# Product of activations and gates moved from VectorE to GpSimd, with each chunk's gathers behind it

## What is computed

```
s = einsum('nhpc,hpkc->nhpk', q, keys32)          # 8 heads, 2 x 128 keys
top_s, top_i = lax.top_k(s, 16)
cand_s = top_s[:, :, 0, :, None] + top_s[:, :, 1, None, :]
best_s, best_c = lax.top_k(cand_s.reshape(n, 8, 256), 16)
expert_idx = take_along_axis(cand_i, best_c)      # 128 experts per position
gate = softmax(best_s)
act = gelu(einsum('nhkd,nd->nhk', expert_u[expert_idx], x_blk))
out = einsum('nhk,nhkd->nd', gate * act, expert_v[expert_idx])
```

## Time and profile before

| what | value |
|---|---|
| median of 3 runs | 1731.21 us (1728.63 to 1732.78) |
| the profiled execution | 1731.74 us |
| its span in the trace | 1730.0 us |
| PE busy | 1696.1 us, 98% of the span |
| DVE busy | 1295.1 us, 75% |
| ACT busy | 774.3 us, 45% |
| POOL busy | 770.5 us, 45% |
| granted clock of TensorE, 1400 to 1500 us | 1.00 |
| DMA share, 1400 to 1500 us | 0.99 |

### The profile page before, as it was taken

The page is one execution under the profiler, slowest core; times in us unless marked ns, Lnnn a source line. Parts: engine busy times, 40 slices in busy tenths (PEclk is TensorE's granted clock), DMA queues, the critical chain, the costliest instruction groups (busy, mean ns, idle before and its releaser), DMA issues.

```text
span 1730.0 us, 24584 instructions
## 1 busy us (share of the span) xinstructions
PE 1696.1 (98%) x9066; PEld 1513.9 (88%) x9066; DVE 1295.1 (75%) x1838; ACT 774.3 (45%) x1101; POOL 770.5 (45%) x486
## 2 busy tenths in 40 slices
PE   7999999989999999999999999999999999999998
PEld 5888788878899999999999999999888888888886
DVE  2555511135999999989999789886787887878886
ACT  5555422333333566756666566654323323223233
POOL 3333243423311556655556678881533433433330
PEclk9999999999999999999999999999999999999999
DMA  5222223322335777687777988898999999999992
GB/s 158 74 73 85 61 82 100 97 73 73 96 119 203 245 243 249 231 287 253 248 253 250 334 310 300 309 308 314 372 380 379 359 362 375 359 362 375 360 378 76
DMA packets 212438, 413.80 MB, mean 239 GB/s; under 512 B 11521, under 2 KB 150817, under 8 KB 207009
## 3 DMA queue, kind: packets, MB, share of 16 engines
q1 hardware_dynamic: 156880, 253.51, 42.4%
q0 software_dynamic: 36864, 134.23, 21.6%
q10 hardware_dynamic: 18640, 25.45, 4.2%
HBM read 360.73 MB, written 52.43 MB: 239 GB/s over the span
## 4 chain that ended last, share of the span: by engine, by line
PE 81%; DVE 9%; POOL 4%; issue 2%; DMA 2%; ACT 1%; ACTq 0%; SPq 0%; POOLq 0%; DVEq 0%
PE psum L1226 30%; PE psum L233 22%; PE psum L1167 20%; PE psum L1157 3%; DVE ring L1500 2%; POOL ring L1384 2%; DVE ul L1425 2%; PE psum L1194 2%; PE psum L308 1%; POOL grid L1403 1%; DVE hot L1488 1%; PE psum L434 1%; POOL hot L1394 1%; DVE hot L1490 1%; DMA ring<-in_expert_u,index 1%
## 5 line engine op out<-in xcount | busy, mean ns | idle before, releaser
L1167 PE MATMUL psum<-xTh,uh 128*128 128x384 f32 x1024 | 354.2, 346 | 5.1 <-DVE ul L1425 4.4
L1167 PE MATMUL psum<-xTh,ul 128*128 128x384 f32 x1024 | 343.3, 335 | 0.0
L1167 PE MATMUL psum<-xTl,uh 128*128 128x384 f32 x1024 | 343.3, 335 | 0.0
L216 POOL TENSOR_TENSOR wl<-raw,wh 128x1024 fp32r<-128x1024 f32 x72 | 173.5, 2420 | 307.1 <-ACT wh L497 307.1
L1384 POOL DMA_INDIRECT ring<-in_expert_v,index x128 | 174.7, 1365 | 296.9 <-DVE acc L1505 253.7
L1226 PE MATMUL psum<-vh,dwh 128*128 128x512 f32 x768 | 298.8, 389 | 1.2 <-DVE dwl L1518 1.2
L1226 PE MATMUL psum<-vh,dwl 128*128 128x512 f32 x768 | 298.8, 389 | 0.0
L1226 PE MATMUL psum<-vl,dwh 128*128 128x512 f32 x768 | 298.8, 389 | 0.0
L1299 ACT ACTIVATE vh<-v_raw 128x4096 fp32r<-128x4096 f32 x31 | 112.6, 3633 | 340.2 <-PE psum L1226 339.8
L1384 POOL DMA_INDIRECT ring<-in_expert_u,index x128 | 178.1, 1391 | 153.2 <-DVE ring L1500 79.5
L1500 DVE SCALAR_TENSOR_TENSOR ring<-ring,x 128x1024 f32<-128x1024 f32 x120 | 199.9, 1678 | 9.3 <-DMA ring<-in_expert_u,index 8.0
(11 more groups left out here) (209 smaller groups left out, 2880.5 us busy)
## 6 DMA issues: line engine op xcount, KB each, us to landing
u_raw<-in_expert_u SPq DMA_DIRECT2D x128, 512.0 KB, 4.8
v_raw<-in_expert_v SPq DMA_DIRECT2D x30, 2048.0 KB, 12.3
expert_act<-hb ACTq DMA_DIRECT2D x128, 192.0 KB, 3.2
expert_gate<-grid SPq DMA_DIRECT2D x12, 2048.0 KB, 7.3
dh<-expert_act SPq DMA_DIRECT2D x32, 768.0 KB, 4.4
dg<-expert_gate SPq DMA_DIRECT2D x32, 768.0 KB, 6.8
raw<-in_w_in SPq DMA_DIRECT2D x40, 512.0 KB, 3.8
raw<-in_w_q SPq DMA_DIRECT2D x16, 512.0 KB, 4.0
```

What stands on the lines that cost most here:

```text
L216: nc.gpsimd.tensor_tensor(wl[slot][:], raw[slot][:], wh[slot][:].bitcast(F), ALU.subtract).then_inc(w_lo[slot], 1)
L1167: last = nc.tensor.matmul(zb[s][:, 0:DT], w[s][:, c, :], x[:, c, 0:DT], start=(c == 0 and i == 0), stop=(c == C - 1 and i == 2))
```

## The change

The function `weights` moves from the DVE program to the POOL program, otherwise word for word. All 32 products are now POOL instructions. On POOL the gathers from number 125 on, which stood in one loop at the end, are dealt out between the products: behind the product of chunk z come the gathers whose slot DVE has freed by the end of its chunk z. The waits of each gather and each product are what they were, and no instruction is added or dropped.

```diff
--- before.py
+++ after.py
@@ -1386,6 +1386,13 @@
                 in_offset=bass.IndirectOffsetOnAxis(ap=index[:, x % SLOTS:x % SLOTS + 1], axis=0),
             ).then_inc(row_in[k], 16)
 
+        def weights(s, r):
+
+            pool.wait_ge(dh_in[s], r * 16 + 16)
+            pool.wait_ge(dg_in[s], r * 16 + 16)
+            w = dh[s][:].rearrange("p j (b n) -> p j b n", n=32)
+            nc.gpsimd.tensor_tensor(w, w, dg[s][:].rearrange("p b j n -> p j b n"), ALU.mult).then_inc(w_f[s], 1)
+
         def lo(k):
             s = k % 2
 
@@ -1415,8 +1422,15 @@
                 gather(GATHER[n])
             if n in HOT:
                 lo(HOT[n])
-        for x in range(RING + rows_done(126), 2 * SLOTS):
+        x = RING + rows_done(126)
+        for z in range(2 * ROUNDS):
+            weights(z % 2, z // 2)
+            while x < 2 * SLOTS and PLAN[x][1] <= rows_done(127 + z):
+                fetch(x)
+                x += 1
+        while x < 2 * SLOTS:
             fetch(x)
+            x += 1
 
     def experts_vector(dve):
         def low(n):
@@ -1516,13 +1530,6 @@
         def weights_lo(s, r):
             dve.wait_ge(w_hi[s], r + 1)
             nc.vector.tensor_tensor(wl[s][:], dh[s][:], wh[s][:].bitcast(F), ALU.subtract).then_inc(w_lo[s], 1)
-
-        def weights(s, r):
-
-            dve.wait_ge(dh_in[s], r * 16 + 16)
-            dve.wait_ge(dg_in[s], r * 16 + 16)
-            w = dh[s][:].rearrange("p j (b n) -> p j b n", n=32)
-            nc.vector.tensor_tensor(w, w, dg[s][:].rearrange("p b j n -> p j b n"), ALU.mult).then_inc(w_f[s], 1)
 
         for n in range(STEPS):
             low(n)
@@ -1558,15 +1565,12 @@
                 row(x)
             if n == STEPS - 3:
                 first_rows_lo(0, S["v_half"])
-            elif n == STEPS - 2:
-                weights(0, 0)
             elif n == STEPS - 1:
                 first_rows_lo(1, v_hi[0]).then_inc(v_lo[0], 1)
         weights_lo(0, 0)
         dve.wait_ge(S["x3_ready"], 2)
 
         for z in range(1, 2 * ROUNDS):
-            weights(z % 2, z // 2)
             rows_lo(z % 2, z // 2)
             weights_lo(z % 2, z // 2)
             if z == 3:
```

## The result

The changed kernel takes 1783.34 us (median of 4 runs, 1780.24 to 1784.83) against 1731.12 us (median of 4). The ratio is 1.0303, with a 95% interval of 1.0291 to 1.0315: 52 us slower. The forecast was 1773 with a range of 1750 to 1788. The profiled execution took 1782.16 us with a span of 1780.4.

What follows compares the result with a forecast made beforehand. PE's down-stage matmuls, 16.33 us a chunk, were taken as the bound. 38.5 us for the cycle in chunks 5 to 30, 1.0 for chunk 4 and 2.3 at the start make 41.8 on 1731.7: about 1773 us, range 1750 to 1788.

Steps and rivals of the forecast that it cites:

- PE's pace in the down stage: Down stage: PE's matmuls set the pace at 16.33 us a chunk, and nobody makes PE wait.
- The product on POOL: One product of 1536 elements on POOL: 3.41 us, with ends of 2.84 and 3.86 us.
- The exclusion: POOL and DVE instructions with two SBUF inputs run one after the other; the second waits for the whole first.
- the gather held by `vl`: A POOL gather issued during `vl` is not done before `vl` ends; its remainder is 0.81 us.
- Rival A: Down stage: gathers don't wait for `vl`, so the cycle is 17.0 us and the time 1751 us; chance 0.1.
- The new cycle: Down stage: rows, `vl` with gather, product, `dwh`, `dwl` in a chain of 17.81 us against PE's 16.33.
- the product-first order: Product ahead of `vl`: pushes `vl` by 0.6 to 2.0 us each chunk until `vl` starts ahead of the last gather.
- Chunk 4: Down stage, chunk 4: `vl` a microsecond late and the gather stuck, making it 1.0 us late for PE.
- the start: Start of the down stage: the first `dwl` waits for chunk 1's product on POOL, 2.3 us onto PE's start.
- the tail: Behind PE's last matmuls: the last block's scaling and way out, short and not touched by the change.
- a slower product: POOL's product at 3.86 us: cycle 18.26 us, sum 55 us, time 1786 us.
- PE was to wait 1 to 2.4 us in nearly each chunk: Sign expected in the changed kernel's profile: PE waits for `dwl` 1 to 2.4 us in nearly each chunk.

Runs made afterwards that it cites:

- the run from chunk 6 on: Changed kernel, but from chunk 6 on the last gather of each chunk stands behind the next product: 1757.23 us, ratio 1.0150.
- the run up to chunk 5: Changed kernel, but up to chunk 5 two gathers of each chunk stand behind the next product: 1772.64 us, ratio 1.0243.
- half the product: Changed kernel with POOL's product on 768 of its 1536 columns, the other weights without gates: 1731.54 us, ratio 1.0009.

## Why the prediction held

**What bounds the kernel.** PE's pace in the down stage: right. The run with almost no product on DVE shows that the relief is worth nothing.

**The product on POOL.** 3.41 predicted, 3.51 measured. The slope between two POOL instructions of other shapes was a fair guide.

**The exclusion, and the gather held by `vl`.** Right, both. The inference of the Trainium skill (SBUF — State Buffer, "Who interferes with whom") that tensor_tensor leaves descriptor generation alone doesn't hold for these indirect gathers: in the changed kernel the last one takes 4.03 us under `vl`, and with `vl` in quarters 0.94. Rival A's cycle of 17.0 us did turn up, at a mean of 17.0, but in the run from chunk 6 on, in which no gather stands between `vl` and the product.

**The new cycle.** 17.81 predicted, 17.97 measured. The 0.16 are the longer product (0.10) and some hundredths of handing over at the other steps, and make some 4 of the 9 us by which the sum came out low. That the product-first order can't hold and gives way in a few chunks was argued in one sentence; the run up to chunk 5 shows it. The run from chunk 6 on shows that the other order, once there, stays for 22 chunks in a program in which the first held from the start.

**Chunk 4 and the start.** 1.0 predicted and 1.1 measured; 2.3 predicted and 2.4 measured.

**What the sum lacked.** Two terms. The start costs not only the wait but also 2.9 us of lower clock behind it; the run with the first two products on POOL shows such a loss too (6.0 us in all). And the tail, which the prediction called untouched, costs 2.6 us. I looked at its length, not at what stands ahead of it on DVE. With these 5.5, the 4.3 of the cycle and 0.2 of the wait and chunk 4, less the 1.4 by which the up stage happened to be shorter, the 41.8 become 50.4. That the 1783 still lies in the range is luck in part: the range reached to 1788 for the sake of a slower product (3.86 us), and the product hardly needed that room. Two losses that the prediction didn't have took it.

**A sign that was only half right.** PE was to wait 1 to 2.4 us in nearly each chunk. The 22 waits of 32.4 us in the table include the 3.62 ahead of chunk 0, so in the cycle it waited 21 times, 28.8 us in all, while its chunks 3 to 30 took 44.0 us more than before. Of the rest, 10.3 us are six chunks of 18.0 us instead of 16.3 that started at a lower clock, and some 0.2 lie around each wait. The cycle is set by DVE, ACT and POOL, so a slower PE costs nothing there, and only hides a wait.

## What to carry to other kernels

Moving an instruction to an engine with idle time doesn't free the first engine if the two exclude each other (and here, with PE setting the pace, freeing it would have brought nothing): count every instruction of the two engines that can shut out another, in the order in which they will be issued. Write down the closed chain (here rows, `vl`, gather, product, `dwh`, `dwl`), add it up, and compare it with the pace of the engine that bounds, for each order in which two neighbours can come. If one order is under the pace and the other over it, the same program can run at two paces, and what came before decides which of them it takes, as the run from chunk 6 on shows. And where a stage starts or ends, look at the clock and at the chain that has been hidden so far: these two were the part of the loss that a sum of cycles didn't give.

## What the hardware did that I had not expected

- The clock at the start of the stage followed the wait ahead of it. Waits of 1.07, 1.21 and 1.87 us ahead of chunk 0 (all but the first two products on POOL, the kernel before, half the product) left the granted clock at 1.00. Waits of 3.62 and 4.83 us (the changed kernel, the first two on POOL) were followed by 0.50 for some six microseconds. The loss did not grow with the wait: over the eight runs with waits of 3.45 to 5.47 us chunk 0 was 1.6 to 2.9 us longer, 2.9 after 3.45 and 1.6 after 5.47.
- In mid-stage the length of the wait alone did not decide. In the changed kernel two waits of 2.14 and 2.16 us (ahead of 1397.50 and 1307.61) were followed by a clock of 1.00, while four of 2.14 to 2.16 us (ahead of 1433.59, 1487.02, 1612.99 and 1702.55) were followed by a mean of 0.58 to 0.68 over 4 us, and two of 2.49 and 2.53 (ahead of 1344.05 and 1559.58) by 0.59 and 0.57. What tells them apart no run here shows.
- The one who waits is served before the one who follows. `dwl`, next in DVE's queue, waited for a product that had been waiting since `vl` (5.06 us instead of 1.75).
- A gather that is held by DVE's instruction ended 0.80 to 0.82 us behind its end, whether the instruction was of 1.75 or of 4.42 us. Behind a `vl` that had itself been pushed by the product it was 0.84 to 0.87 us.
